# Two heads' attention logits on the two row halves of TensorE, and a pair's values one dense product later

## What is computed

```python
def stick_breaking_attention(q, k, v):        # (B, 8, 256, 64)
    z = einsum('bhqd,bhkd->bhqk', qi, k) * dh ** -0.5
    mask = kpos[None, :] < qpos[:, None]
    log_beta = log_sigmoid(z)
    log_rem = where(mask, log_beta - z, 0.0)
    between = cumsum(log_rem, axis=3, reverse=True) - log_rem
    w = where(mask, exp(log_beta + between), 0.0)
    return einsum('bhqk,bhkd->bhqd', w, v)

g_a = sigmoid(gate_sb + bg[:D_MODEL]); g_b = sigmoid(gate_hg + bg[D_MODEL:])
merged = g_a * (o_sb @ w_o_sb) + g_b * (o_hg @ w_o_hg)
h = x + merged @ w_out
```

## Time and profile before

| | |
|---|---|
| median of three runs | 753.24 us (752.58 to 753.93) |
| profiled execution | 752.74 us, its span 750.9 us |
| PE busy | 685.9 us, 91% of the span |
| PEld busy | 527.3 us, 70% |
| DVE busy | 365.0 us, 49% |
| ACT busy | 289.6 us, 39% |
| chain that ended last | PE 71%, DMA 23%, DVE 2%, ACT 1% |
| mean granted TensorE clock | 0.969 |
| read from memory | 208.32 MB |

### The profile page before, as it was taken

The page is one execution under the profiler, slowest core; times in us unless marked ns, Lnnn a source line. Parts: engine busy times, 40 slices in busy tenths (PEclk is TensorE's granted clock), DMA queues, the critical chain, the costliest instruction groups (busy, mean ns, idle before and its releaser), DMA issues.

```text
span 750.9 us, 12901 instructions
## 1 busy us (share of the span) xinstructions
PE 685.9 (91%) x5426; PEld 527.3 (70%) x5426; DVE 365.0 (49%) x577; ACT 289.6 (39%) x423; POOL 48.8 (6%) x84
## 2 busy tenths in 40 slices
PE   3999999999968678677999999999999999999996
PEld 3987878853312122123999989998989899998895
DVE  3667871431110100104867987645875654555543
ACT  4245440241111010004676542668266544344532
POOL 0000000000000000000048750000000000000000
PEclk9999999999988697979999999999999999999999
DMA  8999999999999999999954534430554545664001
GB/s 354 405 414 417 356 425 424 428 425 426 427 427 427 425 427 426 425 425 423 356 194 149 204 124 171 158 112 7 219 206 160 216 150 196 224 224 168 1 0 57
DMA packets 31438, 210.27 MB, mean 280 GB/s; under 512 B 4624, under 2 KB 5008, under 8 KB 6544
## 3 DMA queue, kind: packets, MB, share of 16 engines
q1 hardware_dynamic: 31376, 209.38, 69.1%
HBM read 208.32 MB, written 1.05 MB: 279 GB/s over the span
## 4 chain that ended last, share of the span: by engine, by line
PE 71%; DMA 23%; DVE 2%; SPq 1%; issue 1%; ACT 1%; DVEq 0%
PE psum L423 69%; DMA raw<-in_w_exp 16%; DMA raw<-in_w_in_t 3%; DMA raw<-in_w_in 3%; SPq L465 1%; PE psum L431 1%; DMA raw<-in_w_ada_q 1%; ACT whi L486 0%; DVE X L2461 0%; ACT XT L2408 0%; DVE dT L1001 0%; ACT XH L849 0%; DVE wlo L503 0%; ACT G L1282 0%; DVE xn L991 0%
## 5 line engine op out<-in xcount | busy, mean ns | idle before, releaser
L423 PE MATMUL psum<-XH,whi 128*128 128x256 f32 x736 | 211.3, 287 | 5.3 <-DVE XL L656 2.3
L423 PE MATMUL psum<-XL,whi 128*128 128x256 f32 x736 | 208.2, 283 | 0.0
L423 PE MATMUL psum<-XH,wlo 128*128 128x256 f32 x736 | 208.2, 283 | 0.0
L503 DVE TENSOR_TENSOR wlo<-raw,whi 128x2048 fp32r<-128x2048 f32 (+1 forms) x88 | 168.7, 1957 | 37.4 <-ACT whi L486 37.4
L486 ACT ACTIVATE whi<-raw 128x2048 fp32r<-128x2048 f32 (+1 forms) x79 | 139.3, 1801 | 57.7 <-PE psum L423 37.8
L423 PEld LDWEIGHTS psum<-XH,whi 128*128 128x128 f32 x736 | 141.0, 192 | 10.4 <-issue 5.8
L423 PEld LDWEIGHTS psum<-XL,whi 128*128 128x128 f32 x736 | 141.1, 192 | 0.3
L423 PEld LDWEIGHTS psum<-XH,wlo 128*128 128x128 f32 x736 | 141.0, 192 | 0.0
L423 PE MATMUL psum<-raw,G 128*32 128x512 f32 x456 | 63.4, 675 | 19.4 <-DMA raw<-in_w_exp 11.2
L423 PEld LDWEIGHTS psum<-raw,G 128*32 128x32 f32 x456 | 13.9, 117 | 63.7 <-issue 31.7
L1266 ACT ACTIVATE WT<-psum 128x256 f32<-128x256 f32 x8 | 3.1, 384 | 126.4 <-PE psum L423 92.6
(11 more groups left out here) (350 smaller groups left out, 911.2 us busy)
## 6 DMA issues: line engine op xcount, KB each, us to landing
raw<-in_w_exp SPq DMA_DIRECT2D x88, 1024.0 KB, 25.8
raw<-in_w_ff SPq DMA_DIRECT2D x32, 1024.0 KB, 5.2
raw<-in_w_in SPq DMA_DIRECT2D x22, 1024.0 KB, 7.6
raw<-in_w_ada SPq DMA_DIRECT2D x16, 1024.0 KB, 11.3
raw<-in_w_in_t SPq DMA_DIRECT2D x8, 1024.0 KB, 18.1
X<-in_w_exp SPq DMA_DIRECT2D x6, 1024.0 KB, 26.4
raw<-in_w_ada_q SPq DMA_DIRECT2D x4, 1024.0 KB, 17.1
raw<-in_w_out_t SPq DMA_DIRECT2D x4, 1024.0 KB, 11.5
```

The lines of the kernel that those rows point to most:

```text
L423: return e.matmul(o, l, r, start=start, stop=stop, skip_group_check=True)
L503: e.tensor_tensor(wlo[j % NS][:, x], ring[slot[i]][:, x], whi[j % NS][:, x], ALU.subtract).then_inc(*steps_(("lo", j, x.start // 1024), *[ ...
```

## The change

`pe_z` computes two heads at once: the 256-column matmul of the even head, that of the odd head, then the two 128-column ones, so that neighbours lie on different halves of the rows and write different banks. It takes two banks. It is called for the pairs (2,3), (4,5) and (6,7) in turns 1, 3 and 5 instead of once in each of turns 1 to 6. `zb` has four banks, 0 to 3, and `ob` four, 4 to 7; the ring of the first `o_sb` banks is reordered. The values of pairs 0, 1 and 2 come after the dense product of turns 3, 5 and 7, not ahead of it. ACT's, DVE's, POOL's and SP's lists are the same.

```diff
-            zb, ob, sb_, wb = Banks([0, 1, 2]), Banks([3, 4, 5, 6, 7]), Banks([2, 0, 1, 3]), Banks([4, 5, 6, 7])
+            zb, ob, sb_, wb = Banks([0, 1, 2, 3]), Banks([4, 5, 6, 7]), Banks([0, 1, 2, 3]), Banks([4, 5, 6, 7])
...
                             if hd == 3:
                                 banks = ob
                                 pe_z(e, zb, 0)
-                                pe_z(e, zb, 1)
...
             for i in range(1, 10):
-                if i < 7:
-                    pe_z(e, zb, i + 1)
+                if i in (1, 3, 5):
+                    pe_z(e, zb, i // 2 + 1)
...
-                if i in (3, 5, 7, 9):
-                    pe_sticks(e, banks, i // 2 - 1)
+                if i == 9:
+                    pe_sticks(e, banks, 3)
                 if 1 <= i <= 4:
                     pe_gate(e, banks, w2(18 if i < 3 else 20), 8 if i < 3 else 12, (i - 1) % 2)
                 if 5 <= i <= 8:
                     pe_narrow(e, banks, w2(22 + (i - 5) // 2), (4, 5, 6, 7), (i - 5) % 2, ("o_hg", i - 5))
+                if i in (3, 5, 7):
+                    pe_sticks(e, banks, i // 2 - 1)
...
-        def pe_z(e, banks, h):
-            r, p = slice(64 * (h % 2), 64 * (h % 2) + 64), banks.take(e, ("z", h))
-            if h == 0:
+        def pe_z(e, banks, n):
+            p = [banks.take(e, ("z", 2 * n + r)) for r in range(2)]
+            if n == 0:
                 for q in range(2):
                     e.wait_ge(*at(("sq", "scaled", q)))
                     e.wait_ge(*at(("sk", "scaled", q)))
-            mm(e, p[:, 0:256], sbk[r, h // 2, 0:128], sbq[r, h // 2, 0:256], True, False)
-            mm(e, p[:, 256:384], sbk[r, h // 2, 128:256], sbq[r, h // 2, 128:256], False, False).then_inc(*hyb_pe(("z", h)))
+            for o, w, k in ((0, 256, 0), (256, 128, 128)):
+                for r in range(2):
+                    x = slice(64 * r, 64 * r + 64)
+                    i = mm(e, p[r][:, o:o + w], sbk[x, n, k:k + 128], sbq[x, n, k:256], o == 0, False)
+                    if o:
+                        i.then_inc(*hyb_pe(("z", 2 * n + r)))
```

## The result

The changed kernel takes 759.16 us (median of 6 runs, 758.19 to 762.18), the kernel before beside it 752.69 (751.61 to 753.93). The ratio is 1.0088, 95% interval 1.0073 to 1.0103: **6.6 us slower**, 5.5 to 7.8. Throughout, differences are worked out from such ratios, as (ratio - 1) x 753. The profiled execution took 759.11 us, its span is 757.3 where before's is 750.9.

The account below looks back on a forecast made before the run. PE, busy 91% of the span, was taken to bound the kernel; late values and bank 4 add waits of 8.5 us against 4.6 removed, taken as +3.8: 753.24 + 3.8 = 757.0 us, range 754.6 to 759.6 (forecast's own 755.7 to 758.3).

Parts of the forecast that it names:

- part 1: Logits of heads 2 to 7 in pairs: a pair priced as one head, 3.1 us of PE work gone.
- the old wait: PE's break at 519.16 in the kernel before, 1.03 us in the profile; the cross-check counted about 1.1 to 1.3 gone.
- part 3: Values behind the dense product: late values delay ACT's exponentials and work queued behind them; the sum is +3.8 us.
- steps 1 to 6: Turns 3 to 8: values 0 and 1 delay ACT and DVE; PE waits 1.9 at z6, z7 and 1.6 at values 2.
- part 2: Four banks for logits, four for the rest: values 3 take bank 4 and wait until DVE has read o_hg 3.
- step 7: Values 3: PE comes at 529.8 and waits until 534.5 for bank 4, 4.6 us.
- the rival that its idle time would absorb the lateness: ACT's lateness of 4.6 and 2.3 us absorbed before PE needs it: faster, 748.8 us; chance 0.09.
- The cross-check from PE's side: PE sum over the loop: new waits 8.5 less 4.6 of removed work and old wait, +3.9 us.
- The four waits: PE's new waits: 1.9 at z6, z7, 0.4 for the concatenation, 1.6 before values 2, 4.6 before values 3.
- cheaper switches: PE's switches into and out of the values, counted as 0.3 us of removed work beside the 3.1.
- the fall: Rival: granted clock falls in the gap before values 3, 2.0 us more (0 to 2.6), 759.0 us; chance 0.29.
- the gap of 5.92: Earlier gap ended at 323.76; clock back some 5.3 us after work resumed, priced as 2.6 us lost for dense work.

Follow-up runs that it names:

- pairs in front: Changed kernel with values at their old place ahead of the dense product and last values in bank 5, against the kernel before: ratio 0.9979, -1.6 us.
- only the third pair late: Paired logits, last values in bank 5, only values 2 behind their dense product, against the kernel before: 749.32 us beside 753.48, ratio 0.9955.
- the filled gap: Changed kernel plus 32 thrown-away 128x256 matmuls just before the last values, bank 4 kept: 756.72 us beside 753.48 for the kernel before, ratio 1.0048.
- the first pair late: Paired logits, last values in bank 5, only values 0 behind their dense product, against the kernel before: ratio 0.9990, -0.8 us.

## Why the prediction was right, and where not

**Pairs (part 1)**: three groups of eight records, 0.92 us each (507.55 above is one). The price of one head for two held in all places. Kernels with pairs in front won 1.6 us where 2.1 was worked out; in the profile with only the third pair late, 4.2 us are won up to the last values, of which 1.0 is the old wait and 3.2 work, where 3.1 was given.

**Values behind the product (part 3), steps 1 to 6**: measured against the steps, with 0.2 us of upstream delay in the measured ones. Values 0 at 497.9: 498.15. The late conversions at 499.2: 499.51. Logits 6 and 7 at 507.2: 507.55. First o_hg at 509.5: 509.75. Values 1 at 512.4: 512.79. Values 2 at 522.3: 522.85. ACT's two idle stretches ahead of the exponentials of heads 2 and 4 were given as 4 to 5 and 3 to 4; they are 5.33 and 3.69:

```profile
499.12 0.49 ACT L1824 ACTIVATE xn<-psum 128x384 f32<-128x384 f32 x1 [5.33 <-PE psum L423]
...
506.92 0.49 ACT L1824 ACTIVATE xn<-psum 128x384 f32<-128x384 f32 x1 [1.93 <-DVE psum L2101]
...
513.77 0.49 ACT L1824 ACTIVATE xn<-psum 128x384 f32<-128x384 f32 x1 [3.69 <-PE psum L423]
```

**Bank 4 (part 2, step 7)**: DVE was to read o_hg 3 from 533.7, PE to go on at 534.5:

```profile
529.51 4.48 DVE L503 TENSOR_TENSOR wlo<-raw,whi 128x2048 fp32r<-128x2048 f32 x2
533.91 0.68 DVE L2054 TENSOR_TENSOR gates<-gates,psum 128x512 f32<-128x512 f32 x1
```

It went on at 534.65. PE had come there at 530.55, not at 529.8, so its wait was 4.10 and not 4.6. The same two rows stand at 526.86 and 531.26 in the earlier trace rows, where no one waited for them. The reasoning by order rather than by busy share was what found this: ACT is 38% busy in the changed kernel too, and the rival that its idle time would absorb the lateness failed at each of the three waits.

**The cross-check from PE's side** came out near +3.8 for two wrong terms that cancel. The four waits sum to 7.5 us, not 8.5. The old wait was 1.03, not 1.1 to 1.3. From the first logits to the last values the changed kernel is 3.8 us behind, so the work removed was 7.5 - 1.0 - 3.8 = 2.7 us and not 3.4: the 0.3 for cheaper switches was not there. This is less luck than it looks: the waits end when ACT and DVE let them, so work that PE still has to do only shortens them. Two sums are slightly off by the prediction's own terms: 757.0 + 0.5 + 1.0 is 758.5, not 758.3, and 753.24 - 3.4 - 1.1 is 748.7, not 748.8.

**The clock**: here the forecast chose wrongly. 757.0 was the sum without a fall; the fall had 0.29 and 759.0, and it came. The term was mis-sized as well: I took 2.0 us for it, below the 2.6 of the gap of 5.92, thinking that a shorter gap would give the fall less time afterwards. The profile shows 2.4 and the filled gap 3.0. The time from resuming to the full clock was 5.5 us after a gap of 4.10. With 3.8 and 2.4 the sum is 759.4, against 759.2. The 2.6 for 5.3 us took half of the time as lost, which is too much for work whose starts go from 0.12 to 0.21 us apart. The dense work that I counted against the fall did not prevent it.

**Luck in the number.** The measured 759.16 lies only 0.4 us below the top of the stated range, 759.6. It does so because before ran at 752.69 beside it and not at 753.24, from which I had counted: 753.24 + 6.6 would be 759.8, above the range. The chain of waits was right; that the range holds the result is partly chance, as the forecast itself, +3.8, left out the fall.

## What to carry to other kernels

Before moving an instruction behind another on one engine, list what the other engines have queued behind the waits that it releases, and follow each to the bank or buffer that it frees; a buffer ring that comes round one place earlier can turn a harmless late read into the wait that sets the time. When a ring is resized to serve one product, look at who now shares banks in the others. Look for the longest gap that a change opens: a gap of 4.1 us cost 3.4 by itself and 2.4 to 3.0 again in clock. The move of values paid where it filled a wait that existed (the third pair here); the first pair brought nothing and the second cost 5.0 us against values in front.

## What the runs showed of the hardware that I had not expected

The granted clock also falls behind gaps that are much shorter than the one forecast, and not each time. Five profiles have the same gap of 1.71 us before logits 6 and 7. In two it stayed at 1.00 behind it (the changed kernel, 505 to 519, and the one with the first pair late), in three it fell (the last values in bank 5, the gap filled, DVE reading o_hg 3 first). The changed kernel and the one with the filled gap have the same instructions up to there, so the instructions alone do not decide it. In the profile with the last values in bank 5:

```profile
508.00:509.00 1.00, 1.00 (x9) 0.88 (x10) 0.41 (x2) 0.88 (x2) 0.00 (x0) 1.00 1.03 418
509.00:510.00 1.00, 1.00 (x6) 0.94 (x5) 1.00 (x2) 0.94 (x3) 0.00 (x0) 0.61 1.05 434
510.00:511.00 1.00, 1.00 (x6) 0.99 (x6) 1.00 (x3) 0.38 (x1) 0.00 (x0) 0.50 0.72 303
```

There the fall came 1.4 us after work had resumed at 507.86. With pairs and values in front, it came within a microsecond of the end of a gap of 2.07 us and lasted until 521 (0.50 in 518 to 521). The six falls behind gaps of 1.71 to 4.36 us lasted 3.4 us each, all of it under work; the one in the changed kernel began in its gap of 4.10, 2.8 us after PE had stopped, and lasted 6.8 us, 5.5 of it under work. Before the change, a gap of 1.85 had left the clock up (1.00 in 350 to 360). What decides between the two was not settled; filling the short gaps made no difference that the runs resolve.
